# A two-layer encoder trunk on one core: the last column group taken output tile by output tile

## What is computed

```python
def sq_relu_mlp(xn, w1, w2):
    return jnp.square(jax.nn.relu(xn @ w1)) @ w2
...
        h = h + sq_relu_mlp(rms_norm(h, norm_mlp_g[layer]), mlp_w1[layer], mlp_w2[layer])
    h = rms_norm(h, norm_final_g)
    return h[:, N_META:, :]
```

## Time and profile before

| | |
|---|---|
| median of 3 runs | 2124.24 us (2124.06 to 2124.68) |
| span of the profiled execution | 2122.5 us |
| PE busy | 2098.2 us, 99% |
| DVE busy | 1281.0 us, 60% |
| ACT busy | 927.0 us, 44% |
| POOL busy | 66.0 us, 3% |
| HBM traffic | 383 MB, 180 GB/s over the span |

### The profile page before, as it was taken

How to read it: one execution, slowest core, us unless ns; L and a number is a source line. 1 busy time by engine, 2 the same in 40 slices (tenths; PEclk the granted TensorE clock), 3 DMA queues, 4 the chain that set the end, 5 groups by cost and what they waited for, 6 DMA issues and landing times.

```text
span 2122.5 us, 36370 instructions
## 1 busy us (share of the span) xinstructions
PE 2098.2 (99%) x15226; PEld 1995.2 (94%) x15226; DVE 1281.0 (60%) x1300; ACT 927.0 (44%) x965; POOL 66.0 (3%) x40
## 2 busy tenths in 40 slices
PE   8999999999999999999999999999999999999997
PEld 8999999999999999999999999888888888888886
DVE  8999975445444454555665556665555555555555
ACT  6434464434433433445433333544435434434443
POOL 1001020000000000000100000010000000000001
PEclk9999999999999999999999999999999999999999
DMA  7542455455554555554555555455555554554552
GB/s 281 180 159 100 164 186 187 179 181 187 186 180 178 179 185 187 180 178 178 182 187 186 178 178 185 172 200 195 181 193 183 190 187 178 198 183 177 195 195 79
DMA packets 55336, 383.91 MB, mean 181 GB/s; under 512 B 6176, under 2 KB 8224, under 8 KB 9312
## 3 DMA queue, kind: packets, MB, share of 16 engines
q1 hardware_dynamic: 54880, 381.84, 50.2%
q0 software_dynamic: 240, 1.02, 0.1%
q10 hardware_dynamic: 144, 0.04, 0.0%
HBM read 380.78 MB, written 2.10 MB: 180 GB/s over the span
## 4 chain that ended last, share of the span: by engine, by line
PE 96%; DVE 2%; ACT 1%; issue 0%; DMA 0%; DVEq 0%; SPq 0%
PE banks L320 25%; PE banks L314 19%; PE banks L313 19%; PE banks L312 19%; PE banks L322 13%; DVE wl L805 1%; ACT wh L529 0%; DVE h L833 0%; ACT xs L546 0%; DMA raw<-weights 0%; DVE ssum L943 0%; DVE h L1157 0%; DVE h L1163 0%; ACT sq L556 0%; PE banks L447 0%
## 5 line engine op out<-in xcount | busy, mean ns | idle before, releaser
L805 DVE TENSOR_TENSOR wl<-raw,wh 128x1024 fp32r<-128x1024 f32 x720 | 892.0, 1250 | 728.7 <-ACT wh L529 728.1
L529 ACT ACTIVATE wh<-raw 128x1024 fp32r<-128x1024 f32 x720 | 753.7, 1058 | 977.8 <-PE banks L314 616.5
L312 PE MATMUL banks<-xs,wh 128*128 128x258 f32 (+1 forms) x2176 | 619.6, 285 | 10.0 <-DVE wl L805 10.0
L314 PE MATMUL banks<-xs,wl 128*128 128x258 f32 (+1 forms) x2176 | 619.4, 285 | 0.0
L313 PE MATMUL banks<-xs,wh 128*128 128x258 f32 (+1 forms) x2176 | 618.1, 284 | 0.0
L320 PE MATMUL banks<-hid,wh 128*128 128x512 f32 x1280 | 449.0, 394 | 0.0
L312 PEld LDWEIGHTS banks<-xs,wh 128*128 128x128 f32 x2176 | 410.1, 188 | 10.3 <-issue 8.7
L313 PEld LDWEIGHTS banks<-xs,wh 128*128 128x128 f32 x2176 | 410.9, 189 | 0.1
L314 PEld LDWEIGHTS banks<-xs,wl 128*128 128x128 f32 x2176 | 410.4, 189 | 0.0
L312 PE MATMUL banks<-hid,wh 128*128 128x258 f32 x1280 | 362.6, 283 | 1.4 <-DVE hid L849 1.4
L314 PE MATMUL banks<-hid,wl 128*128 128x258 f32 x1280 | 362.2, 283 | 0.0
(11 more groups left out here) (103 smaller groups left out, 779.6 us busy)
## 6 DMA issues: line engine op xcount, KB each, us to landing
raw<-weights SPq DMA_DIRECT2D x359, 1024.0 KB, 4.8
out<-h SPq DMA_DIRECT2D x8, 256.0 KB, 2.7
h<-x SPq DMA_DIRECT2D x3, 544.0 KB, 11.3
raw<-weights SPq DMA_DIRECT2D x2, 512.0 KB, 6.3
conv<-dft_seq POOLq DMA_DIRECT2D x1, 580.5 KB, 12.4
h<-x SPq DMA_DIRECT2D x2, 272.0 KB, 4.5
act<-dft_ch POOLq DMA_DIRECT2D x1, 258.0 KB, 8.1
par<-params POOLq DMA_DIRECT2D x1, 160.0 KB, 6.3
```

The source lines that it names most:

```text
L312: pe.matmul(dst, w[0], v[0], start=start, stop=False)
L314: return pe.matmul(dst, w[1], v[0], start=False, stop=stop)
L529: act.activation(wh[:, j % RING, :, :], src.rearrange("p (t c) -> p t c", t=SLAB_K), ACT.Copy).then_inc(high_ready, 1)
L805: dve.tensor_tensor(wl[:, j % RING, :, :], src.rearrange("p (t c) -> p t c", t=SLAB_K), wh[:, j % RING, :, :].bitcast(F32), ALU.subtract). ...
```

## The change

It touches the last quarter of the last MLP and the final norm.

- Weights: the last group's four chunks hold one output tile each, with all its 16 input tiles (`weight_chunks`). A slab is half of such a chunk, 8 input tiles for one output tile. Their number and size stay.
- TensorE: the last quarter stands outside the loop over quarters, and its last group is `last_group`. Slabs 0 and 1 fill the first of the four banks, slabs 2 and 3 the second, and so on. The sums over channels, five matmuls by `ones`, stand behind slab 3 (square of tile 0), slab 5 (`ssum` and tile 1), slab 7 (tile 2), and at the very end (tile 3).
- VectorE: `tail_add(m)` adds one tile in two halves. `tail_add(0)` stands behind the split of slab 5, `tail_add(1)` behind that of slab 7, the other two after it.
- ScalarE: `tail_square(m)` squares one tile and, for the first three, multiplies it in place by the gain. The first stands ahead of slab 7's high part.
- Final multiplications: tiles 0 to 11 four at a time, 12 to 14 as three, 15 singly with its gain; stores in the same pieces, that of tiles 12 to 14 from ScalarE's queue, the others from SyncE's.

```diff
+FINAL_TILES = ((0, 4), (4, 8), (8, 12), (12, 15), (15, 16))
+LAST_STORES = ((12, 15),)
...
-            for n in range(KT // 2):
-                sp.wait_ge(normed, 2 * n + 2)
-                sp.dma_start(out[:, 2 * n:2 * n + 2, :], h[:, 2 * n:2 * n + 2, FROM2:]).then_inc(stored, 16)
+            for t0, t1 in FINAL_TILES:
+                if (t0, t1) in LAST_STORES:
+                    continue
+                sp.wait_ge(normed, t1)
+                sp.dma_start(out[:, t0:t1, :], h[:, t0:t1, FROM2:]).then_inc(stored, 16)
...
+            def tail_total(m):
+                pe.wait_ge(tail_sq, m + 1)
+                return pe.matmul(banks[:, 0, 0:N2], ones[:, :], sq4[:, m, FROM2:], start=m == 0, stop=m == M - 1)
+
+            def last_group():
+                pe.wait_ge(banks_free, G_END - 2)
+                for s in range(SLABS):
+                    pe.wait_ge(low_ready, S_END - SLABS + s + 1)
+                    m, slot = s // 2, s % RING
+                    for i in range(KT // 2):
+                        k = KT // 2 * (s % 2) + i
+                        t, cols = i // M, slice(P * (i % M), P * (i % M) + P)
+                        last = wide_product(banks[:, M + m, :], (wh[:, slot, t, cols], wl[:, slot, t, cols]),
+                                            (hid[:, 0, k, FROM2:], hid[:, :, k, FROM2:]), k == 0, k == KT - 1)
+                    last.then_inc(slab_used, 1)
+                    if s == 3:
+                        pe.wait_ge(banks_free, G_END - 1)
+                        tail_total(0)
+                    elif s == 5:
+                        pe.wait_ge(ssum_ready, 2 * 4 + 2)
+                        pe.matmul(banks[:, 0, 0:N2], ones[:, :], ssum[:, 0, FROM2:], start=False, stop=False)
+                        tail_total(1)
+                    elif s == 7:
+                        tail_total(2)
+                tail_total(M - 1).then_inc(total_ready, 1)
...
+            def tail_square(m):
+                t = KT - M + m
+                if m == 0:
+                    act.wait_ge(summed, 4 * (KT // M - 1) + 2)
+                act.wait_ge(joined, 4 * QUARTERS + m + 1)
+                act.activation(sq4[:, m, FROM2:], h[:, t, FROM2:], ACT.Square).then_inc(tail_sq, 1)
+                if m < M - 1:
+                    act.wait_ge(tail_sq, m + 1)
+                    act.activation(h[:, t, FROM2:], h[:, t, FROM2:], ACT.Copy, scale=gain(4, t)).then_inc(scaled, 1)
...
+                        if g == GQ - 1 and last and next_norm == 4:
+                            slabs(s0, SLABS * g + E, SLABS * g + SLABS - 1)
+                            tail_square(0)
+                            slabs(s0, SLABS * g + SLABS - 1, SLABS * g + SLABS)
...
+            def tail_add(m):
+                t = KT - M + m
+                group_done(S_END - SLABS + 2 * m + 2, G_END - 1)
+                dve.tensor_tensor(h[:, t, FROM2:], h[:, t, FROM2:], banks[:, M + m, N2:2 * N2],
+                                  ALU.add).then_inc(tail_added, 1)
+                dve.wait_ge(tail_added, m + 1)
+                dve.tensor_tensor(h[:, t, FROM2:], h[:, t, FROM2:], banks[:, M + m, 0:N2],
+                                  ALU.add).then_inc(joined, 1)
...
+                        if g == GQ - 1 and last and next_norm == 4:
+                            slabs(s0, SLABS * g + E, SLABS * g + E + 2)
+                            tail_add(0)
+                            slabs(s0, SLABS * g + E + 2, SLABS * g + SLABS)
+                            tail_add(1)
...
+            tail_add(2)
+            tail_add(3)
             reciprocal(4, FROM2)
-            for t in range(0, KT - M, 2):
...
+            for t0, t1 in FINAL_TILES[:-1]:
+                dve.wait_ge(scaled, t1)
+                dve.tensor_tensor(h[:, t0:t1, FROM2:], h[:, t0:t1, FROM2:], over(rstd, t1 - t0, FROM2),
+                                  ALU.mult).then_inc(normed, t1 - t0)
+            t = KT - 1
+            dve.scalar_tensor_tensor(h[:, t, FROM2:], h[:, t, FROM2:], gain(4, t), rstd[:, FROM2:],
+                                     ALU.mult, ALU.mult).then_inc(normed, 1)
...
+    last = mlp_w2[1][DFF - D:, D - COLS:].reshape(KT, P, M, P).transpose(2, 1, 0, 3)
+    out[-1] = last.reshape(M, P, CHUNK_K * COLS)
```

More of the change, by code:

```diff
@@ L237, in _ @@
                     load_chunk(r * RAW + slot, slot, True)
-            for n in range(KT // 2):
-                sp.wait_ge(normed, 2 * n + 2)
-                sp.dma_start(out[:, 2 * n:2 * n + 2, :], h[:, 2 * n:2 * n + 2, FROM2:]).then_inc(stored, 16)
-            sp.wait_ge(stored, 16 * (KT // 2))
+            for t0, t1 in FINAL_TILES:
[3 more added lines that the diff above has]
+                sp.dma_start(out[:, t0:t1, :], h[:, t0:t1, FROM2:]).then_inc(stored, 16)
+            sp.wait_ge(stored, 16 * len(FINAL_TILES))
         @block.gpsimd
@@ L395, in hid_phase, with mlp @@
                               par_, hid, lo, ready=ready)
-            def mlp(slab0, index0, norm, lo, hid0):
+            def mlp(slab0, index0, norm, lo, hid0, final=False):
                 x_phase(slab0, index0, 2, norm, lo)
@@ L400, in mlp @@
                           lambda s: s % 2 == 0 and pe.wait_ge(hid_ready, hid0 + s // 2 + 1))
-                with pe.Fori(1, QUARTERS) as q:
+                with pe.Fori(1, QUARTERS - 1 if final else QUARTERS) as q:
                     with pe.Fori(0, 2) as i:
@@ L411, in mlp @@
                                       hid_ready, q * 4 + (hid0 + s // 2 + 1)))
+                if final:
+                    q = QUARTERS - 1
+                    with pe.Fori(0, 2) as i:
+                        for par_ in range(2):
+                            group(i * (2 * SLABS) + (q * SQ + slab0 + SLABS * par_),
+                                  i * 2 + (q * GQ + index0 + par_), par_, xs4, lo)
+                    for g in range(3):
+                        group(q * SQ + slab0 + SQ // 2 + SLABS * g, q * GQ + index0 + GQ // 2 + g, g % 2,
+                              hid, lo, ready=lambda s: s % 2 == 0 and pe.wait_ge(
+                                  hid_ready, q * 4 + hid0 + s // 2 + 1))
+                    last_group()
             def channel_dft(hd):
@@ L510, in _ @@
                       lambda s: s % 2 == 0 and pe.wait_ge(gated_ready, s // 2 + 1))
-            mlp(S_MLP1, G_MLP1, 3, FROM2, QUARTERS * 4)
-            final_total()
+            mlp(S_MLP1, G_MLP1, 3, FROM2, QUARTERS * 4, final=True)
         @block.scalar
@@ L750, in quarter @@
                                                    scale=gain(4, t)).then_inc(scaled, 1)
-                        slabs(s0, SLABS * g + E, SLABS * g + SLABS)
+                        if g == GQ - 1 and last and next_norm == 4:
+                            slabs(s0, SLABS * g + E, SLABS * g + SLABS - 1)
+                            tail_square(0)
+                            slabs(s0, SLABS * g + SLABS - 1, SLABS * g + SLABS)
+                        else:
+                            slabs(s0, SLABS * g + E, SLABS * g + SLABS)
                         if g == 0 and first:
@@ L790, in _ @@
             mlp(S_MLP1, 3, FROM2, G_MLP1, 4 * QUARTERS, 4, FROM2)
[L791 to L795, removed]
+            for m in range(1, M):
+                tail_square(m)
             norm_root(4, FROM2)
+            for t0, t1 in LAST_STORES:
+                act.wait_ge(normed, t1)
+                act.dma_start(out[:, t0:t1, :], h[:, t0:t1, FROM2:]).then_inc(stored, 16)
         @block.vector
@@ L1149, in _ @@
             mlp(S_MLP1, 3, FROM2, G_MLP1, 4 * QUARTERS, 4, FROM2, FROM2)
[L1151 to L1159, removed]
-            reciprocal(4, FROM2)
-            for t in range(0, KT - M, 2):
[L1162 to L1167, removed]
+            tail_add(2)
+            tail_add(3)
+            reciprocal(4, FROM2)
+            for t0, t1 in FINAL_TILES[:-1]:
[5 more added lines that the diff above has]
+                                     ALU.mult, ALU.mult).then_inc(normed, 1)
 def dft_tables():
```

## The result

The changed kernel takes 2128.50 us, the median of 14 runs (2127.81 to 2129.09), and the kernel before 2124.45 beside it. The ratio is 1.0020, 95% interval 1.0013 to 1.0027: slower by about 4 us, at the edge of what I had called no change, and above my range of 2125.0 to 2127.9.

What follows compares the result with a forecast made beforehand. TensorE's products were taken to set the pace, then a serial chain up to the stores. 3.25 + 0.86 - 2.30 + 0.53 = +2.34 us on 2124.24 gave 2126.6 us, range 2125.0 to 2127.9.

Steps and rivals of the forecast that it cites:

- The stall costs the clock: Rival: TensorE's 2.55 us idle time behind slab 3 halves its clock, losing 2.36 us, time 2129.0; chance 0.07.
- Term A: TensorE behind slab 3: waiting for tile 0's square and doing the first sum costs +3.25 us, 0.43 of it the sum.
- B: TensorE behind slab 5: the sums over `ssum` and tile 1's square cost +0.86 us, without a stall.
- C: Chain from the last product to the root: shortened from 4.44 to 2.14 us, -2.30 us.
- D: First final multiplication, now four tiles wide: grows from 0.69 to 1.22 us and delays the first store, +0.53 us.
- part 5: Final multiplications and stores: the end hangs on the first store, not the last, as stores flow at 357 GB/s.
- The splits aren't held up: Rival: VectorE splits slabs 4 and 5 at 1.22 us each, the stall is 1.0 us, time 2125.1; chance 0.05.
- No stall at all: Rival: tile 0's square is ready before TensorE needs it behind slab 3, leaving 0.43 us, time 2123.8; chance 0.01.

## Why the prediction was wrong

- **What failed is the rival "The stall costs the clock", which I gave 0.07.** It is what happened. My sum put nothing for the granted clock behind the wait. I placed an idle time of 2.55 us between 1.58, after which the clock had stayed, and the 4.7 at the end, over which it stayed too before it fell, and took the 4.7 as a sign that 2.55 is too short. It is none, because the delay of the fall is not fixed. The changed kernel's last matmul ends at 2115.35, and there the clock is down by 2116.2, not after 4.7 us (busy time by stretch):

```profile
2115.40:2116.00 0.60, 0.00 (x0) 0.00 (x0) 0.12 (x1) 0.45 (x1) 0.00 (x0) 1.00 0.00 0
2116.20:2117.00 0.80, 0.00 (x0) 0.00 (x0) 0.80 (x1) 0.00 (x0) 0.00 (x0) 0.50 0.00 0
```

The rows of the kernel before left the case open, and an open case isn't 0.07. The fall cost 1.53 us by the traces and 1.1 to 1.4 by the medians, for the 2.36 of the rival: it lasted 3.42 us of the trace, not the 5.12 of the slow stretch at the start.

- **Term A was 3.74 us for 3.25.** The mechanism was right to the instruction: the place, both slow splits, the adds (0.41 and 0.42 for 0.43), and the folds as their cause. What is over is the square's start, 0.38 us behind the add for 0.03, and the sum's, 0.14 behind the square for 0.04. The other three squares start 0.03 to 0.04 behind their adds, as the last one in the chain above does (2113.72 + 0.43 to 2114.17). The late one is there in every variant that has it between the slabs, 0.37 or 0.38 behind its add. It waits for a second semaphore (`summed`), but so does the first square of the kernel before, which starts 0.09 behind its add (2108.79 to 2108.88). No run moves it, so its cause stays open.
- **Terms B, C and D** came out at 0.86, -2.29 and +0.53 for 0.86, -2.30 and +0.53. The stores are the end, as part 5 has it; between first store and end another 0.2 us appeared, not looked into.
- **The rival "The splits aren't held up"** gave 2125.1; the kernel in which they aren't took 2125.42. The rival "No stall at all" gave 2123.8 for sums in place; with a sum behind slab 5 there was still a small stall and 2124.57.
- **Why a change that shortens the chain by 2.3 us loses 4:** it buys this with 3.7 + 0.9 us and 1.5 us of half clock on the engine that sets the pace for the whole kernel, while the same engine stands idle a few us later; the wider first piece adds 0.5.

The version with all sums behind slab 7 and the first four tiles in twos beats both kernels: 2121.93 us, 2.3 below the one before (interval 0.9980 to 0.9998) and 6.6 below the changed one.

## What to carry to other kernels

A piece of the end that is moved ahead belongs where its engine is idle, not merely where its input may be ready: here the sums cost 0.43 us each between products and nothing behind the last one. In a list that runs strictly in order, work out when each input arrives, stalls of its producers by a third engine included, and again after each stall you take out. An idle time on TensorE that is longer than any after which the trace shows it going on at full clock is to be priced with the half clock, at a chance that counts: by the times it fell in some six of eleven executions behind 2.49 us, and in 24 of 25 behind 3.00. When the bytes of the last stores flow at a flat rate, make the first piece small and leave the rest wide; here two tiles were enough, and one gave nothing more.

## What was not expected of the hardware

- The granted clock of TensorE (1.00, 2.4 GHz) fell to 0.50 (1.2 GHz) right behind 3.00 us without a matmul, and was up again by 2102.42; after 2.49 us it stayed in the profiled execution, and the times say that it did not in all; after 1.47 us it stayed. Behind the last matmul it had fallen within 0.9 us in the changed kernel, while in the one before it stayed for 4.7. The Trainium skill, "TensorE: Matmul & The Clock Gate", Part 1, has an idle TensorE back at half its clock, and the moment at which the clock rises vary from run to run; these runs agree with the first and show that the moment of the fall varies too.
- A ScalarE square that waits for VectorE started 0.38 us behind the add in one place and 0.03 to 0.04 in three others.
- Six matmuls whose result is overwritten made a kernel 1.4 us faster by the medians, 1.5 by the traces.
